# Two transformer blocks on one core: another order of the first loads and sums, gate sums in two parts, bias strips a head ahead

## The reference

```python
# first block
mod = silu(c) @ w_ada + b_ada                      # c: one row of 2048; w_ada: 2048 x 6144
shift, scale, gate = split(mod, 3)
h = rms(x, norm_g) * (1 + scale) + shift           # needs all of shift and scale
a_q, a_k, a_v, a_z, g_q, g_f, g_i, g_z = split(h @ w_in)
att = chunk_attention(a_q, a_k, a_v, bias) * silu(a_z)       # 8 heads, a bias strip for each
hg  = hgrn2(g_q, g_f, g_i, lb) * silu(g_z)                   # 8 heads, a gated recurrence
x = x + gate * (concat(att, hg) @ w_out)           # the first use of gate
# second block: memory attention (c), sliding window (b) and top-k attention (a), each gated
m_k, m_v = split(rms(mem) @ w_mem)                 # 256 memory rows
x = x + (g_a*(oa @ w_up_a) + g_b*(ob @ w_up_b) + g_c*(oc @ w_up_c)) @ w_o
```

## Time and profile before

| what | value |
|---|---|
| median of three runs | 2750.07 us |
| the profiled execution | 2751.61 us |
| its span, first to last instruction | 2750.3 us |
| TensorE matmul busy | 2680.7 us (97%) |
| VectorE (DVE), ScalarE (ACT), GpSimd (POOL) busy | 35%, 38%, 42% |
| DMA, mean over the span | 118 GB/s |
| mean granted TensorE clock | 0.991 |

### The profile page before, as it was taken

One profiled execution on the slowest core, in us unless ns is written; L12 is line 12 of the kernel. 1 busy time (PEld: TensorE's weight loads), 2 busy tenths in 40 slices (PEclk: granted clock), 3 DMA queues, 4 the chain that ended last, 5 costly groups with the idle time before them and its releaser, 6 DMA issues.

```text
span 2750.3 us, 31306 instructions
## 1 busy us (share of the span) xinstructions
PE 2680.7 (97%) x12574; PEld 2154.7 (78%) x12574; DVE 971.3 (35%) x1557; ACT 1048.3 (38%) x1684; POOL 1157.4 (42%) x587
## 2 busy tenths in 40 slices
PE   6899999999999999999999999999999999999999
PEld 4567888887777778878888777777888888888787
DVE  3525544443243322134567333334222223212300
ACT  5234333333333433234443444445444344333311
POOL 0013333334434445453334434444555555545543
PEclk9999999999999999999999999999999999999999
DMA  9741222223433223432222223223333333333443
GB/s 372 295 172 69 70 71 75 77 100 119 153 116 129 104 84 134 147 118 85 77 77 85 92 96 104 96 96 102 104 106 115 104 111 117 115 117 113 136 139 110
DMA packets 102096, 323.27 MB, mean 118 GB/s; under 512 B 11328, under 2 KB 12864, under 8 KB 101440
## 3 DMA queue, kind: packets, MB, share of 16 engines
q1 hardware_dynamic: 98208, 307.64, 32.2%
q10 hardware_dynamic: 3744, 13.63, 1.3%
HBM read 304.45 MB, written 16.78 MB: 117 GB/s over the span
## 4 chain that ended last, share of the span: by engine, by line
PE 90%; DVE 3%; DMA 3%; POOL 1%; ACT 1%; SPq 1%; issue 1%; ACTq 0%; DVEq 0%
PE bank L758 26%; PE bank L759 26%; PE bank L760 26%; PE bank L880 2%; DMA TA<-in_w_ada 2%; PE bank L957 1%; POOL wlo L2016 1%; PE bank L946 1%; DMA TA<-in_strip 1%; PE bank L663 1%; PE bank L808 1%; DVE TA L1801 1%; PE bank L940 1%; ACT whi L1061 1%; PE bank L911 1%
## 5 line engine op out<-in xcount | busy, mean ns | idle before, releaser
L2016 POOL TENSOR_TENSOR wlo<-wraw,whi 128x1024 fp32r<-128x1024 f32 (+3 forms) x430 | 993.6, 2312 | 1448.2 <-ACT whi L1061 1447.3
L758 PE MATMUL bank<-Hhi,whi 128*128 128x512 f32 x2928 | 1198.9, 409 | 11.8 <-DVE Hlo L1557 4.1
L759 PE MATMUL bank<-Hlo,whi 128*128 128x512 f32 x2928 | 1147.2, 392 | 0.0
L760 PE MATMUL bank<-Hhi,wlo 128*128 128x512 f32 x2928 | 1146.9, 392 | 0.0
L1061 ACT ACTIVATE whi<-wraw 128x1024 fp32r<-128x1024 f32 (+2 forms) x454 | 456.8, 1007 | 683.0 <-PE bank L760 655.5
L758 PEld LDWEIGHTS bank<-Hhi,whi 128*128 128x128 f32 x2928 | 553.1, 189 | 154.6 <-issue 36.6
L759 PEld LDWEIGHTS bank<-Hlo,whi 128*128 128x128 f32 x2928 | 553.7, 189 | 119.0 <-issue 11.4
L760 PEld LDWEIGHTS bank<-Hhi,wlo 128*128 128x128 f32 x2928 | 552.3, 189 | 119.7
L758 PE MATMUL bank<-Ohi,whi 128*128 128x512 f32 x320 | 128.0, 400 | 0.0
L760 PE MATMUL bank<-Ohi,wlo 128*128 128x512 f32 x320 | 124.8, 390 | 0.0
L759 PE MATMUL bank<-Olo,whi 128*128 128x512 f32 x320 | 124.7, 390 | 0.0
(11 more groups left out here) (259 smaller groups left out, 2460.0 us busy)
## 6 DMA issues: line engine op xcount, KB each, us to landing
wraw<-in_w_in SPq DMA_DIRECT2D x304, 512.0 KB, 3.2
TA<-in_w_ada SPq DMA_DIRECT2D x64, 512.0 KB, 6.9
first<-in_w_ada SPq DMA_DIRECT2D x32, 512.0 KB, 4.4
wraw<-in_w_out SPq DMA_DIRECT2D x32, 512.0 KB, 3.2
wraw<-in_w_o SPq DMA_DIRECT2D x32, 512.0 KB, 3.2
wraw<-in_w_mem ACTq DMA_DIRECT2D x16, 512.0 KB, 7.0
tmp_mgs<-TA SPq DMA_DIRECT2D x32, 256.0 KB, 2.1
TA<-tmp_mgs SPq DMA_DIRECT2D x32, 256.0 KB, 3.6
```

What stands on the lines that cost most here:

```text
L758: e.matmul(out, hi[:, c], xhi[k], start=first and j == 0, stop=False)
L759: e.matmul(out, hi[:, c], xlo[k], start=False, stop=False)
L760: m = e.matmul(out, lo[:, c], xhi[k], start=False, stop=last and end)
L2016: e.tensor_tensor(M.wlo[b][:, 0:w], M.wraw[b][:, 0:w], M.whi[b][:, 0:w].bitcast(F32), ALU.subtract).then_inc(S.lo)
```

## The change

It has three parts.

**The start.** `START` takes four `m` ahead of the first `a`, and so on, and ends with a8; each of the first five begun tiles has one ada group, the sixth has two, and two tiles follow them. `normed` is called in `mem` 13 and 14 and in `ada(9)` and `ada(10)`. The mask copy moves from `ada(10)` to `ada(13)`.

**The gate.** `gates(g)` is called for each half. The first half stands in `slow` ahead of head 0's tiles and takes two sums in each slot; its tiles are loaded into four places in the first half of x's memory (Y), which is free once h's low half is made. Then come `mem_turn` and the second half, with one sum in 12 slots and the old three places.

**The strips.** Strip h+1 is loaded in head h's step, in all three attentions; the first one in the step of hg(7) (behind hg(6)), the first two of b in that of the memory attention's head 0, the first of a in window 5.

```diff
-START = "m0 m1 a0 m2 m3 a1 m4 m5 m6 a2 m7 m8 a3 m9 m10 s0 a4 m11 m12 a5 m13 a6 a7 m14 s1 m15"
-BEGUN = ((48, 3, ()), (41, 2, (8,)), (56, 4, (9,)), (33, 5, (10,)), (49, 1, (11,)), (57, 0, (12, 13)), (40, 7, (14, 15)),
+START = "m0 m1 m2 m3 a0 m4 m5 a1 m6 m7 a2 m8 m9 a3 m10 m11 s0 a4 m12 a5 m13 a6 a7 m14 s1 m15 a8"
+BEGUN = ((48, 3, (9,)), (41, 2, (10,)), (56, 4, (11,)), (33, 5, (12,)), (49, 1, (13,)), (57, 0, (14, 15)), (40, 7, ()),
          (32, 6, ()))
+GATE_PACE = ((1, 2), (12, 1))
+def gate_steps(g):
+    slots, pieces = GATE_PACE[g]
+    return slots * KT // pieces
...
+        self.gate_slot = (pieces(Y, 0, 4, 1024), (first[:, 0:1024], first[:, 1024:2048], first[:, 3072:4096]))
... in_order
+    beat.add("slow", do["gates"](0))
+    beat.add("slow", do["mem_turn"]())
+    beat.add("slow", do["gates"](1))
     for h in range(8):
...
-                if h == 0:
-                    beat.add("slow", do["mem_turn"]())
                 beat.add("core", do["hg"](h))
-    beat.add("slow", do["gates"]())
... TensorE
+    def gates(g):
+        yield from rest(gate_steps(g))
+        pe.wait_ge(S.adm, KT * (g + 1))
+        pe.wait_ge(*free[BVV])
... DVE: mem and ada
-        if k >= 13:
+        if k in (13, 14):
             normed(4 * k - 52)
-        if q == 8:
-            normed(12)
-        if q == 10:
+        if q in (9, 10):
+            normed(4 * q - 28)
+        if q == 13:
... DVE
+    def gates(g):
+        (slots, share), places, landed = GATE_PACE[g], M.gate_slot[g], S.adg[g]
+        for j in range(KT):
+            i, c = j % len(places), M.par[:, 64 + j:65 + j]
+            dve.wait_ge(landed[i], 16 * (j // len(places) + 1))
...              tensor_scalar for j == 0, else scalar_tensor_tensor behind the last one, as before
+            if j % share == share - 1:
+                yield from rest(slots)
... SP
+    def gates(g):
+        (slots, share), places, landed = GATE_PACE[g], M.gate_slot[g], S.adg[g]
+        ahead = len(places)
+        def one(j):
+            if j < KT:
+                if j >= ahead:
+                    sp.wait_ge(S.adm, KT * g + j - ahead + 1)
+                e.dma_start(places[j % ahead], io["w_ada"][4 + g, j]).then_inc(landed[j % ahead], 16)
+        if g == 0:
+            sp.wait_ge(S.phi, KT + 8)
+            sp.wait_ge(S.plv, KT + 8)
+        else:
+            sp.wait_ge(S.adc, 4)
+            sp.wait_ge(S.mask8, 1)
+        for j in range(ahead):
+            one(j)
+        for first in range(0, KT, share):
+            yield from rest(slots)
+            for j in range(first, first + share):
+                one(j + ahead)
+        yield
+    def hg(h):
+        if h == 7:
+            sp.wait_ge(S.hgu, 9 * 7)
+            strip(1, 0)
+        return rest(11)
... SP, attend
-            if which == 1:
-                sp.wait_ge(*((S.s1, 4 * (h - 1)) if h > 1 else (S.hgu, 9 * (7 + h))))
-                e.dma_start(M.W1["ST"][h % 2], io["strip1"][h]).then_inc(S.strip[h % 2], 16)
+            if which == 1 and h < 7:
+                sp.wait_ge(*((S.s1, 4 * h) if h else (S.hgu, 9 * 8)))
+                strip(1, h + 1)
```

More of the change, by code:

```diff
@@ L51 @@
 PLACES = 8
-START = [(x[0], int(x[1:])) for x in "m0 m1 a0 m2 m3 a1 m4 m5 m6 a2 m7 m8 a3 m9 m10 s0 a4 m11 m12 a5 m13 a6 a7 m14 s1 m15".split()]
-BEGUN = ((48, 3, ()), (41, 2, (8,)), (56, 4, (9,)), (33, 5, (10,)), (49, 1, (11,)), (57, 0, (12, 13)), (40, 7, (14, 15)),
+START = [(x[0], int(x[1:])) for x in ("m0 m1 m2 m3 a0 m4 m5 a1 m6 m7 a2 m8 m9 a3 m10 m11 s0 a4 m12 a5 m13 a6 a7 "
+                                      "m14 s1 m15 a8").split()]
+BEGUN = ((48, 3, (9,)), (41, 2, (10,)), (56, 4, (11,)), (33, 5, (12,)), (49, 1, (13,)), (57, 0, (14, 15)), (40, 7, ()),
          (32, 6, ()))
+GATE_PACE = ((1, 2), (12, 1))
 LOW, HIGH = range(8), range(8, 16)
@@ L287, in __init__ @@
         self.sel = self.par[:, 105:106]
-        self.gate_slot = (first[:, 0:1024], first[:, 1024:2048], first[:, 3072:4096])
+        self.gate_slot = (pieces(Y, 0, 4, 1024), (first[:, 0:1024], first[:, 1024:2048], first[:, 3072:4096]))
         self.gate_acc = first[:, 4096:5120]
@@ L365, in __init__ @@
         self.mem, self.x = many("mem", 4), many("xin", 4)
-        self.ada, self.adg = many("ada", PLACES), many("adg", 3)
+        self.ada, self.adg = many("ada", PLACES), (many("adg", 4), many("adh", 3))
         self.raw = many("raw", NRING)
@@ L418 @@
 MEM_BANKS = (1, 0, BS1, BT)
-GATE_SLOTS = 3
 def in_order(beat, do):
@@ L782, in moved @@
         return (S.eva, n["eva"]) if kind in BY_ACT else (S.evd, n["evd"])
[L784 to L793, removed]
+    def gates(g):
+        yield from rest(gate_steps(g))
+        pe.wait_ge(S.adm, KT * (g + 1))
+        pe.wait_ge(*free[BVV])
+        for i in range(8):
+            m = e.matmul(M.bV[:, i:i + 1], M.gate_acc[:, i * P:(i + 1) * P], ones[:, 0:1], start=True, stop=True)
+        m.then_inc(S.adc)
+        free[BVV] = (S.adp, 5 + g)
+        yield
     def silu(*at):
@@ L1200, in moved @@
         return (S.eva, n["eva"]) if kind in BY_ACT else (S.evd, n["evd"])
-    def gates():
-        yield from rest(2 * (16 * GATE_SLOTS + 1))
+    def gates(g):
+        return rest(gate_steps(g) + 1)
     def chain(x, bias=0.0):
@@ L1620, in out @@
             e.tensor_tensor(M.u[nb % 2], src, M.lb[nb % 2], ALU.add).then_inc(S.out)
[L1622 to L1640, removed]
+    def gates(g):
[3 more added lines that the diff above has]
+            dve.wait_ge(landed[i], 16 * (j // len(places) + 1))
+            if j == 0:
+                dve.wait_ge(S.adc, 4 + g)
+                e.tensor_scalar(M.gate_acc, places[i], c, None, ALU.mult).then_inc(S.adm)
+            else:
+                dve.wait_ge(S.adm, KT * g + j)
+                e.scalar_tensor_tensor(out=M.gate_acc, in0=places[i], scalar=c, in1=M.gate_acc, op0=ALU.mult,
+                                       op1=ALU.add).then_inc(S.adm)
+            if j % share == share - 1:
+                yield from rest(slots)
+        dve.wait_ge(S.adc, 5 + g)
+        cc = 4 + g
+        e.tensor_tensor(M.par[:, 8 * cc:8 * cc + 8], M.bV[:, 0:8], M.c("b_ada", 8 * cc, 8), ALU.add).then_inc(S.adp)
+        n.up("adp")
+        yield
     def minus(x, bias=0.0):
@@ L2155, in part, with gates, strip @@
         beat.steps(x, ks)
[L2157 to L2171, removed]
+    def gates(g):
+        (slots, share), places, landed = GATE_PACE[g], M.gate_slot[g], S.adg[g]
[8 more added lines that the diff above has]
+            sp.wait_ge(S.plv, KT + 8)
+        else:
+            sp.wait_ge(S.adc, 4)
[6 more added lines that the diff above has]
+                one(j + ahead)
+        yield
+    def strip(which, h):
+        W, name = (M.W1, "strip1") if which == 1 else (M.W2, "strip_" + which)
+        e.dma_start(W["ST"][h % 2], io[name][h]).then_inc(S.strip[h % 2], 16)
+    def hg(h):
[3 more added lines that the diff above has]
+        return rest(11)
     def attend(which, h):
@@ L2178, in run @@
         def run():
-            if which == 1:
-                sp.wait_ge(*((S.s1, 4 * (h - 1)) if h > 1 else (S.hgu, 9 * (7 + h))))
-                e.dma_start(M.W1["ST"][h % 2], io["strip1"][h]).then_inc(S.strip[h % 2], 16)
-            elif which == "a":
-                sp.wait_ge(S.s1, g0 - 4)
-                e.dma_start(M.W2["ST"][h % 2], io["strip_a"][h]).then_inc(S.strip[h % 2], 16)
+            if which == 1 and h < 7:
+                sp.wait_ge(*((S.s1, 4 * h) if h else (S.hgu, 9 * 8)))
+                strip(1, h + 1)
+            elif which == "c" and h == 0:
+                sp.wait_ge(S.x1s, 16 * KT)
+                sp.wait_ge(S.evd, 1)
+                strip("b", 0)
+                strip("b", 1)
+            elif which == "a" and h < 5:
+                sp.wait_ge(S.s1, g0)
+                strip("a", h + 1)
             yield from rest(att_steps(a))
@@ L2192, in run @@
         def run():
[L2193 to L2197, removed]
+            if h:
+                sp.wait_ge(S.s1, g0)
+                strip(*(("b", h + 1) if h < 5 else ("a", 0)))
             yield from rest(WINDOW_STEPS)
@@ L2244, in sync_program @@
         setup=setup, mem=mem, mem_kv=idle(3), mem_turn=idle(2), ada=nothing, sums=nothing, gain=nothing, h_put=nothing,
-        gates=gates, hg=idle(11), attend=attend, window=window,
+        gates=gates, hg=hg, attend=attend, window=window,
         put=nothing, x_load=x_load, h2=nothing, index=idle(3), topk=idle(48), mix_load=mix_load, out_load=out_load,
```

## The result

The changed kernel takes 2744.18 us (median of 18 runs, 2741.99 to 2746.89), the kernel before 2751.07 us (18 runs). The ratio is 0.9975, 95% interval 0.9968 to 0.9982: 6.9 us or 0.25% faster. I had forecast 2740.7, by terms that come to 9.4 us. By the bound of 0.3% the result counts as no change, a case to which I gave 0.36, though the interval excludes a ratio of 1.

What follows compares the result with a forecast made beforehand. TensorE, busy for 97% of the span, was taken as the bound, with only idle and half-clock time to win. Terms -17 + 21 + 2 - 15.4 = -9.4 us gave 2742.2 profiled and a median of 2740.7; range 2724 to 2755.

Steps and rivals of the forecast that it cites:

- the bound of 0.3%: Whole kernel: 0.3% (8.3 us) is about what a measurement tells from no change; faster needs less than 2741.8 us.
- a case to which I gave 0.36: Whole kernel: the time counts as the same, neither faster nor slower by 0.3%; chance 0.36.
- Start: Up to item 24: reordered m steps and ada groups cut TensorE's waits and cold clock, gaining 17 us (bounds 10 and 22).
- a sign of being wrong: Wrong if the last ada group is not under 150 us, or TensorE stands less than 12 us in head 0.
- The term for a7: In the start: ada group a7 starts at 87.5 us, 5.4 us earlier, and a wait of 4.7 us stays.
- My third rival: In the start: a7's wait is only moved and returns at a15; gain 6 instead of 17, 2752 us; chance 0.13.
- Head 0: Beside head 0: sixteen gate sums in DVE's queue make TensorE wait, costing 21 us with the cold clock (11 to 44).
- The sixteen sums with what POOL adds: In head 0: DVE's sums take 21 us one after another, and blocking by POOL's instructions adds 8.5 us.
- Second half: The gate's other sums, one in 12 slots: eight lie beside hg of heads 0 to 7, costing 2 us (0 to 8).
- Strips: First block's attention: loading a head ahead removes 13.0 us of waits and two cold stretches, gaining 15.4 us (6 to 17).
- The fourth rival: In the attention: POOL blocking a scaling could make the long waits without late strips; gain 6, 2750 us; chance 0.05.
- The forecast of faster: Whole kernel: less than 2741.8 us; chance 0.55.

Runs made afterwards that it cites:

- old_m_order: The changed kernel with the old order of m and a up to a7 and the new end of the start: 2746.05 us, ratio 0.9979.
- quarter_sums: The changed kernel with the sums of the gate's first half over 256 of 1024 columns, the others left out: 2737.94 us, ratio 0.9959.
- early_loads: The changed kernel with the gate's first four tiles loaded right behind the last ada tile: 2738.88 us, ratio 0.9953.
- pace22: The changed kernel with the gate's first half at two sums in two slots, over heads 0 and 1: 2736.78 us, ratio 0.9950.
- pace66: The changed kernel with both halves of the gate at one sum in six slots: 2722.32 us, ratio 0.9893.
- strips_only: The kernel before with strips loaded a head ahead alone, start and gate as before: 2732.07 us, ratio 0.9927.
- start_strips: The kernel before with the new start and the strips a head ahead, gate as before: 2722.9 us, ratio 0.9903.
- start_only: The kernel before with the new order of the start alone, gate and strips as before: 2740.32 us, ratio 0.9958.

## Why the prediction was nearly right

**Start: forecast 17 us, measured 8 (6.8 in the changed kernel's profile).** This is the step that failed: "The new one has 58.6 - 5.7 = 52.9 us of work there and reaches a7 at 82.8." It is also what the forecast itself named as a sign of being wrong: the last ada group was to be under 150 us and is at 152.00. Of the places that were to show it, a7 is at 94.69 instead of 87 to 88, the last ada group at 152 instead of 142, and item 24 at 178 instead of 168. I charged the early weight tiles to a0 (1.3 us) and let a1 come without a wait. But with two m steps more done before a1, 1.83 MB more of weights are fetched ahead of its tiles in a DMA that is full until 45 us, so that a1 comes 6 us later; the idle time that m2 and m3 filled is paid there (old_m_order shows it moved back). The term for a7 (5.4 us) was therefore nil: a7 came 1.8 us later than before. The 9.5 us from a5's end to a7's start were right: 94.69 less a5's end at 85.4 is 9.3. From a7 to the last begun tile the forecast was 71.9 us (176.4 - 17, less 87.5) against 83.5 before; it took 74.9 (169.63 - 94.69), so that 8.6 of the 11.6 us forecast there came. My third rival (gain 6, 2752 in all) had the right reason, that a7's wait is moved, and nearly the right size; its total of 2752 was off because the strips gave more.

**Head 0: forecast 21 us, measured 20** (between item 24 and the anchors 314.38 and 327.72: 20.1). Waits of 18 to 20 us in total were forecast, 19.35 came. The first sum was to start 10.7 us after item 24 (195.5 on the old axis) and started at 10.8; the sixteenth was to end 44.7 us after it and ended at 43.7. The terms inside were less exact. The sixteen sums with what POOL adds were to take 29.5 us (21 and 8.5) and took 26.4; for their tiles they were not to wait at all, and waited 3.1 (2.02, 0.57 and 0.50). The gate's columns were put at 0.9 us; they take 1.84 at the full clock in the attention of the kernel before, and 3.54 here, behind a wait. Against that, the old waits of 3.8 us in this stretch are gone, of which the forecast counted 2.0. The errors cancel.

The mechanism was incomplete, too: I added up DVE's queue and took the loads alone to end at 33 us. quarter_sums, with DVE's sums 0.48 us long instead of 1.28, ends at 38 and keeps 14.6 us of wait; early_loads, with the first loads out of the head, keeps 13.5. I read this as two chains of nearly one length that lie side by side, since taking away either gives back less than a third; no run takes away both and leaves the density. What is shown is that the density makes the wait: pace22 leaves 11.4 us of it, and in pace66 both waits are gone.

By the Trainium skill, "SBUF — State Buffer", section "SBUF: two separate sides", a DVE instruction with two SBUF inputs and a GpSimd one that reads SBUF block each other wholly. The trace nearly agrees: four sums of 1.28 us took 7.33 us around one remainder, where the times added up are 7.5 (5.1 and 2.39), and 8.17 around a remainder and a SiLU product, where they are 8.8 (with 1.29); a remainder of 2.39 us became 3.34 among the sums.

**Second half: forecast +2, measured +2.6** (from 314.38 and 327.72 to 588.50 and 604.42), of which 1.5 are small waits of 0.4 us each (5.4 against 3.9 in all). None of the 1.4 us that I had allowed for came.

**Strips: forecast 15.4, measured 18 alone, 20.9 from the third step of hg(7) on in the changed kernel.** All 13.0 us went and the cold stretches with them, which cost 5.0 us and not the 3.4 of the forecast; the 1 us that I left for sums blocked by POOL was not needed. The fourth rival is refuted. The other 2.8 us of the 20.9 aren't the strips': the columns of the gate's first half moved out of the attention into head 0, where the forecast and the 20.1 above count them, and hg(7)'s wait of 1.36 us is 0.43. The columns in the kernel before:

```profile
766.09 1.84 PE L790 MATMUL bank<-cst,first 128*128 128x1 f32 x16
```

**The sum** came out near because the start's missing 10 us (17 against 6.8) and the attention's 5.5 in excess (20.9 against 15.4) have opposite signs: -6.8 + 20.1 + 2.6 - 20.9 is the -5.0 of the profiled executions. That the total is within 4 us is luck to this extent. The forecast of faster rested on a difference of one us to the bound, and it isn't borne out.

## What to carry to other kernels

Where work is moved under another engine's busy stretch, write down the queue of each engine in that stretch in order, and find what the waiting engine has queued behind it; the gate sums were free in the attention, and free as well when spread thinly from head 0 on (pace66), but cost about 20 us when sixteen of them stood dense beside head 0. A load that is issued by a queue which trails the consumer can cost up to its landing time on a use (here 3.7 us at most, 13.0 over the heads, and 5 more by the clock), and was here the cheapest thing to move. When the DMA is full, filling one gap with work that asks for more bytes moves the gap; count the bytes ahead of the next wait before taking credit.

## What the runs showed of the hardware that I had not expected

The same instructions with the same waits ran at two granted clocks in head 0. Stretches from the last begun tile to mem_turn and on to hg's wait of 1.5 us, first of the kernel before, then of strips_only, which is the same program there:

```profile
176.40:212.80 36.40, 34.37 (x145) 28.21 (x145) 16.89 (x27) 18.14 (x27) 15.50 (x7) 0.92 0.23 80
212.80:230.60 17.80, 16.31 (x80) 13.57 (x81) 8.79 (x13) 8.25 (x13) 6.05 (x3) 0.90 0.13 46
```

```profile
177.60:212.60 35.00, 32.97 (x144) 27.22 (x145) 17.05 (x27) 18.15 (x27) 15.48 (x7) 0.95 0.26 83
212.60:228.90 16.30, 14.75 (x81) 12.48 (x81) 8.84 (x13) 8.26 (x13) 6.07 (x3) 1.00 0.14 49
```

The granted clock is 0.92 and 0.90 in one and 0.95 and 1.00 in the other, with the same wait of 2.02 us ahead of mem_turn in both. That is 36.4 + 17.8 against 35.0 + 16.3 us, 2.9 us in all. start_strips (0.92, 0.90) goes with the first, start_only (0.95, 1.00) with the second. What decides it isn't shown. It need not be the kernel: of the five executions of strips_only two had a mean granted clock of 0.992 over the whole span and took 2734.1 and 2734.2 us, the other three 0.994 and 0.995 and 2730.0 to 2732.1. The 2.9 us are two fifths of the changed kernel's whole gain of 6.9 us, and a reason to trust anchors in a trace only to about 3 us.
